# The first layer's gate third of the conditioning matrix: loaded and multiplied inside the in-projection instead of the prologue

## Chip, cores and metric

The kernel runs on one core of a Trainium2 chip. The metric is the device time of one execution in microseconds (us); the program is one launch, and the figures below are of executions of it. TensorE is called PE here, VectorE DVE, ScalarE ACT, GpSimd POOL, and SyncE, which issues the loads, SP.

## What is computed

One inference step of a four-layer decoder: 512 prompt tokens and 8 sample tokens, width 1024. Every layer is a token mixer (layers 0 and 3: a gated short convolution) and a gated convolution FFN. Each of the two is wrapped in norms that are steered by a conditioning vector of 9 sequences:

```
mod = jnp.einsum('bd,lde->lbe', jax.nn.silu(c), p['ada_w']) + p['ada_b'][:, None, :]
...
sh_m, sc_m, gt_m, sh_f, sc_f, gt_f = jnp.split(mod[l][:, None, :], N_MOD, axis=-1)
u = rmsnorm(h, p['norm_g'][l, 0]) * (1 + sc_m) + sh_m
...
out, nb = short_conv_mixer(u, st_conv_a[j], p['sconv_w_in'][j], p['sconv_conv_w'][j],
                           p['sconv_w_out'][j])
...
h = h + gt_m * rmsnorm(out, p['norm_g'][l, 1])
```

So of the matrix half that belongs to a layer's mixer, shift and scale (`sh_m`, `sc_m`) are needed before the layer's first matmul, and the gate (`gt_m`) only after its out-projection.

## The kernel before

**The conditioning matrix.** `ada_w` is 1024 rows by 6144 columns for each layer, in f32. A half of it (3072 columns, index h from 0 to 7) serves one sub-layer, a third of a half is 1024 columns: shift, scale or gate. The half h = 0 is needed first of all and is handled in the prologue: SP issues six loads of 2 MB (`ada_pro`, line 546), each 512 columns wide, and PE multiplies each as it comes (line 1782, 32 matmuls of 128 columns a step, steps 0 to 5). A step's sums go through DVE (`mod_rows`, line 2565) and back through a small PE matmul (line 1788) into `ada_ps` in PSUM. Between these steps PE also forms the statistics of the first norm (line 1717), and turns the vectors of biases and gains, which DVE copies to `vecs` (lines 2568 and 2569). Then `modulation(0, 0, mod_m)` adds bias and gain on DVE (lines 2535, 2537, 2542).

**The other halves** come in pieces of 128 rows by 1024 columns (512 KB), two to a pair, into a buffer `ada_raw` that holds one pair. A pair costs PE 8 matmuls (line 1628). Eight pieces, four pairs, make one third; then ACT copies the sums out of PSUM (`copy_sums`, line 1029, into `acc_sb`) and PE turns them into `ada_ps` (`turn_sums`, line 1621) before the next third's first pair. The half h = 1 (12 pairs) is spread over the in-projection of layer 0.

**The in-projection** ("sconv") of layer 0 multiplies 24 blocks of weights, 1024 by 128 each, called B0 to B23 here, with the normed input, in 4 iterations of two tiles (e = 0 and 1) of 3 blocks. A block is loaded by SP into one of two slots of `w_raw` (`load_block`, line 504), copied by ACT to `w_hi` (`high`, line 981), subtracted by POOL to `w_lo` (`low`, line 765; in parts for the first two, line 772), and then multiplied on PE: high parts (line 1667), low part (line 1675). B0 and B1 are multiplied together, as the normed input comes out of ACT and DVE (`gemm_pair`, lines 1690 and 1696).

**What sets the order.** Each engine runs its own list of instructions in order, and waits at the head of it. On SP a load of a pair waits until PE has used the pair before it (`ada_used`), and a load of a block waits until POOL is done with the block two before it (`lo_done`). On PE `conv_tile` places the pairs behind blocks: one pair behind each odd block, so B1, B3, B5 and so on. On ACT `conv_tile` copies the sums behind the weight copy that the pair is near to (`sums_behind`).

## Time and profile before

| | |
|---|---|
| median of 3 runs | 3019.37 us (3018.94 to 3023.8) |
| span of the profiled execution | 3014.3 us |
| PE busy | 2876.1 us, 95% of the span |
| weight loads on PE (PEld) busy | 2733.3 us, 91% |
| DVE, ACT, POOL busy | 51%, 36%, 44% |
| DMA | 332.56 MB, 110 GB/s on average |

The span runs from the first instruction to the last of one execution; the median lies 5.1 us above it. Times in rows are microseconds from the start of that span. PE is the engine that is full almost everywhere; the change concerns the first 210 us, where the profile shows the prologue (to about 53 us) and the in-projection of layer 0 (to about 210 us).

### The profile page before, as it was taken

What the parts mean: (1) busy time and instruction counts of PE and PEld (TensorE: products, weight loads), DVE (VectorE), ACT (ScalarE), POOL (GpSimd) and SP (SyncE); (2) the same over time, 40 slices, a digit from 0 to 9 for tenths busy, and PEclk for the clock granted to TensorE, in tenths of its full rate; (3) what the DMA queues carried; (4) which work ended last, traced back from release to release, by engine and by line L of the source; (5) the groups of instructions that cost most, each with busy time, mean ns of one, the idle gap of its engine ahead of it and who ended that gap; (6) DMA issues with size and microseconds to landing.
All of it is one profiled execution on the core that took longest, in us unless ns stands there. A gap on an engine that the chain in (4) does not pass through costs nothing.

```text
span 3014.3 us, 72962 instructions
## 1 busy us (share of the span) xinstructions
PE 2876.1 (95%) x29617; PEld 2733.3 (91%) x29617; DVE 1528.4 (51%) x2080; ACT 1085.0 (36%) x2139; POOL 1321.5 (44%) x959
## 2 busy tenths in 40 slices
PE   6999999998989999999998999999999999899998
PEld 5998999997978877899997899889999899799998
DVE  3435666118357874666603242476650444566612
ACT  4224333225455652433323444343332422433322
POOL 3443444442435554344443273434444344344443
PEclk9999999999999999999999999999999999899999
DMA  7544333544411013333354323533334543133332
GB/s 269 164 151 159 95 92 88 158 128 136 119 44 32 4 37 124 120 89 92 99 159 152 99 64 112 169 123 89 92 116 146 173 120 91 57 92 92 91 91 85
DMA packets 465618, 332.56 MB, mean 110 GB/s; under 512 B 19914, under 2 KB 435608, under 8 KB 465122
## 3 DMA queue, kind: packets, MB, share of 16 engines
q1 hardware_dynamic: 461400, 325.24, 35.1%
q10 hardware_dynamic: 4010, 4.22, 0.6%
q8 instruction: 172, 2.82, 0.4%
q14 instruction: 36, 0.29, 0.0%
HBM read 319.62 MB, written 10.20 MB: 109 GB/s over the span
## 4 chain that ended last, share of the span: by engine, by line
PE 62%; DVE 4%; ACT 2%; issue 1%; DMA 1%; SPq 0%; POOL 0%; ACTq 0%; DVEq 0%
PE banks L1667 33%; PE banks L1675 16%; PE banks L2126 5%; PE banks L2133 1%; PE banks L1628 1%; PE banks L1973 1%; DVE h L2662 1%; PE banks L1690 1%; DVE proj L2606 1%; PE banks L1761 0%; DMA s_state<-in_state_wkv_b_dram 0%; ACT conv L1080 0%; PE banks L2135 0%; ACT uv L1433 0%; DVE proj_b L2606 0%
## 5 line engine op out<-in xcount | busy, mean ns | idle before, releaser
L765 POOL TENSOR_TENSOR w_lo<-w_raw,w_hi 128x1024 fp32r<-128x1024 f32 x395 | 1007.5, 2551 | 1108.1 <-ACT w_hi L981 1088.0
L1667 PE MATMUL banks<-u_hi,w_hi 128*128 128x260 f32 x4064 | 834.5, 287 | 14.2 <-ACT w_hi L981 9.4
L1667 PE MATMUL banks<-u_lo,w_hi 128*128 128x260 f32 x4064 | 825.1, 284 | 0.0
L1667 PEld LDWEIGHTS banks<-u_hi,w_hi 128*128 128x128 f32 x4064 | 627.4, 189 | 27.1 <-issue 15.2
L1667 PEld LDWEIGHTS banks<-u_lo,w_hi 128*128 128x128 f32 x4064 | 629.9, 189 | 1.6
L981 ACT ACTIVATE w_hi<-w_raw 128x1024 fp32r<-128x1024 f32 x402 | 424.5, 1056 | 454.2 <-PE banks L1675 284.4
L1675 PE MATMUL banks<-u_hi,w_lo 128*128 128x260 f32 x4064 | 527.5, 282 | 0.0
L1675 PEld LDWEIGHTS banks<-u_hi,w_lo 128*128 128x128 f32 x4064 | 502.1, 187 | 1.3
L1667 PE MATMUL banks<-hid_hi,w_hi 128*128 128x260 f32 x1664 | 336.3, 283 | 0.0
L1667 PE MATMUL banks<-hid_lo,w_hi 128*128 128x260 f32 x1664 | 335.2, 283 | 0.0
L3113 DVE TENSOR_TENSOR csb<-proj 128x520 f32 (+1 forms) x42 | 30.3, 722 | 470.8 <-ACT proj L1048 470.8
L2594 DVE TENSOR_TENSOR hid_lo<-prod,hid_hi 128x520 f32 x104 | 259.7, 2497 | 12.8
L1667 PEld LDWEIGHTS banks<-hid_hi,w_hi 128*128 128x128 f32 x1664 | 256.8, 188 | 5.0 <-issue 3.7
L2578 DVE SCALAR_TENSOR_TENSOR conv<-gate,vecs,conv 128x536 f32<-128x536 f32 x104 | 249.2, 2396 | 15.1 <-DVE conv L2576 0.8
L1667 PEld LDWEIGHTS banks<-hid_lo,w_hi 128*128 128x128 f32 x1664 | 256.1, 188 | 0.0
L1675 PE MATMUL banks<-hid_hi,w_lo 128*128 128x260 f32 x1664 | 217.0, 282 | 0.0
L1675 PEld LDWEIGHTS banks<-hid_hi,w_lo 128*128 128x128 f32 x1664 | 206.4, 188 | 0.0
L780 POOL TENSOR_TENSOR tail<-gate,ones 128x2 f32<-128x2 f32 x104 | 28.0, 269 | 339.1 <-ACT gate L1536 339.1
L1543 ACT ACTIVATE conv<-conv,vecs 128x536 f32<-128x536 f32 x88 | 65.5, 744 | 287.5 <-DVE conv L2578 287.5
L2575 DVE TENSOR_SCALAR conv<-gate,vecs 128x536 f32<-128x536 f32 x104 | 55.9, 538 | 194.5 <-ACT gate L1536 190.5
L1534 ACT ACTIVATE gate<-banks 128x260 f32<-128x260 f32 x88 | 34.1, 387 | 256.2 <-PE banks L1675 254.8
L2576 DVE SCALAR_TENSOR_TENSOR conv<-gate,vecs,conv 128x536 f32<-128x536 f32 x104 | 108.1, 1039 | 15.2 <-DVE conv L2575 1.7
(463 smaller groups left out, 3898.8 us busy)
## 6 DMA issues: line engine op xcount, KB each, us to landing
w_raw<-in_ffn_w_up_dram SPq DMA_DIRECT2D x176, 512.0 KB, 3.7
ada_raw<-in_ada_w_dram SPq DMA_DIRECT2D x96, 512.0 KB, 4.7
w_raw<-in_ffn_w_down_dram SPq DMA_DIRECT2D x64, 448.0 KB, 3.7
w_raw<-in_sconv_w_in_dram SPq DMA_DIRECT2D x48, 512.0 KB, 5.2
ada_ahead<-in_ada_w_dram SPq DMA_DIRECT2D x36, 512.0 KB, 7.7
ada_ahead_down<-in_ada_w_dram SPq DMA_DIRECT2D x36, 512.0 KB, 6.2
w_raw<-in_ffn_w_down_dram SPq DMA_DIRECT2D x32, 512.0 KB, 4.0
ada_pro<-in_ada_w_dram SPq DMA_DIRECT2D x6, 2048.0 KB, 21.2
```

Of the source, the lines that this page charges most:

```text
L765: pool.tensor_tensor(w_lo[:, s, :, :], w_raw[:, s, :, :], w_hi[:, s, :, :].bitcast(F32), ALU.subtract).then_inc(lo_done, 1)
L981: act.activation(w_hi[:, s, :, :], w_raw[:, s, :, :], ACT.Copy).then_inc(hi_done, 1)
L1534: act.activation(gate[:, e, 2:2 + HALF], tile_ps[0][0][:, 0:HALF], ACT.Copy)
L1543: act.activation(conv[:, e, 0:CWD], conv[:, e, 0:CWD], ACT.Silu, bias=vec("ffn_conv_b", l * FT + m)).then_inc(silu_done, 1)
L1667: pe.matmul(tile_ps[slot][half][0:width, 0:HALF], w_hi[:, s, k, 0:width], x[:, k0 + k, half * HALF:(half + 1) * HALF], start=start and k = ...
L1675: mm = pe.matmul(tile_ps[slot][half][0:width, 0:HALF], w_lo[:, s, k, 0:width], xh[:, k0 + k, half * HALF:(half + 1) * HALF], start=False, ...
L2126: mm = pe.matmul(out(rs), left(rs), right(rs), start=start, stop=stop)
L2575: link(dve.tensor_scalar(conv[:, e, 0:CWD], gate[:, e, 0:CWD], w[0], None, ALU.mult))
L2576: link(dve.scalar_tensor_tensor(conv[:, e, 0:CWD], gate[:, e, 1:1 + CWD], w[1], conv[:, e, 0:CWD], ALU.mult, ALU.add))
L2578: dve.scalar_tensor_tensor(conv[:, e, 0:CWD], gate[:, e, 2:2 + CWD], w[2], conv[:, e, 0:CWD], ALU.mult, ALU.add).then_inc(conv_done, 1)
L2594: dve.tensor_tensor(lo, prod[:, e, :], hi.bitcast(F32), ALU.subtract).then_inc(hid_ready, 1)
L3113: return dve.tensor_tensor(csb[:, 1, :], o, o, ALU.mult)
```

## The change

Of the half h = 0 the prologue now loads and multiplies only shift and scale (four steps instead of six). The gate third is cut into pieces like the other halves: four more pairs, called P0 to P3 here, go through `ada_raw`; the twelve pairs of h = 1 are P4 to P15. The in-projection of layer 0 now places a pair behind the first block of each iteration and behind each odd block: four pairs an iteration. ACT copies a third's sums at the end of each iteration. The gate's sums are turned into PSUM bank 7 and finished on DVE after the in-projection.

```diff
@@ prologue
+PRO_STEPS = 2 * KT // PRO_T
...
-            for i in range(GT // PRO_T):
-                if i == len(ada_pro):
-                    sp.wait_ge(pro_mod_mm, 1)
+            for i in range(PRO_STEPS):
                 sp.dma_start(ada_pro[i % len(ada_pro)][:, :, :], w[:, :, i * PRO_T * P:(i + 1) * PRO_T * P])\
                   .then_inc(ada_pro_loaded[i], 16)
@@ SP
+            def load_first_gate(x):
+
+                for s in range(2):
+                    i = 2 * KT + 2 * x + s
+                    sp.wait_ge(ada_used, i + 1)
+                    sp.dma_start(ada_raw[:, s, :], ada_columns(0, i)).then_inc(ada_loaded[s], 16)
...
                                 load_block(n0 + 6 * it + k, k % 2, w[:, :, ds((part * KT + m) * P, P)])
...
-                                if k % 2:
-                                    load_ada_slot(p, 3 * it + k // 2)
+                                if l:
+                                    if k % 2:
+                                        load_ada_slot(p, 3 * it + k // 2)
+                                elif k == 0 or k % 2:
+                                    x = 4 * it + (k + 1) // 2
+                                    if x < FIRST_GATE:
+                                        load_first_gate(x)
+                                    else:
+                                        load_ada_slot(p, x - FIRST_GATE)
@@ ACT, conv_tile
                             high(n + i, (k + i) % 2)
-                            if i == 3 - e:
+                            if l and i == 3 - e:
                                 sums_behind(p, 3 * it + e)
-                        if e:
+                        if l and e:
                             sums_behind(p, 3 * it + 2)
+                        if l == 0 and e:
+                            copy_sums(it - 1)
                         rows_to_dram(q, q0 // 2 + it, e,
@@ PE
-            pe.sem_inc(ada_used, 2 + GT)
+            pe.sem_inc(ada_used, 2 + 2 * KT)
...
             def turn_sums(group, first_tile):
-                pe.wait_ge(acc_copied, group + 1)
+                pe.wait_ge(acc_copied, group + 2)
+                sums = first_gate_ps if group < 0 else ada_ps
...
-            for i in range(GT // PRO_T + 1):
+            for i in range(PRO_STEPS + 1):
...
-                            if k % 2:
-                                ada_slot(p, 3 * it + k // 2)
+                            if l:
+                                if k % 2:
+                                    ada_slot(p, 3 * it + k // 2)
+                            elif k == 0 or k % 2:
+                                first_layer_slot(4 * it + (k + 1) // 2)
                         turn_tail(q, e)
+
+                    def first_layer_slot(x):
+
+                        if x < FIRST_GATE:
+                            for s in range(2):
+                                pe.wait_ge(ada_loaded[s], 16 * x + 16)
+                                ada_columns(ada_raw[:, s, :], 2 * x + s)
+                        else:
+                            if x == FIRST_GATE:
+                                pe.wait_ge(rows_copied, q0 + 3)
+                            ada_slot(p, x - FIRST_GATE)
@@ DVE
-            modulation(0, 0, mod_m)
+            def first_modulation():
+
+                dve.wait_ge(mod_mm, 2 * KT)
+                bias = vecs[:, col["ada_b"]:col["ada_b"] + 2 * KT].unsqueeze(2).to_broadcast([P, 2 * KT, NSEQ])
+                gain = vecs[:, col["norm_g"]:col["norm_g"] + KT].unsqueeze(2).to_broadcast([P, KT, NSEQ])
+                scale = mod_m[:, KT:2 * KT, :]
+                link(dve.tensor_tensor(mod_m[:, 0:2 * KT, :], ada_ps[:, 0:2 * KT * NSEQ].rearrange("p (t s) -> p t s", s=NSEQ),
+                                       bias, ALU.add))
+                link(dve.tensor_scalar(scale, scale, 1.0, None, ALU.add))
+                dve.tensor_tensor(scale, scale, gain, ALU.mult).then_inc(mod_ready, 1)
+                dve.wait_ge(mod_ready, 1)
+
+            def first_gate():
+
+                dve.wait_ge(mod_mm, GT)
+                dve.wait_ge(rows_copied, KT + 1)
...
+                link(dve.tensor_tensor(gate_rows, gate_rows, gain, ALU.mult))
+
+            first_modulation()
...
                     after_loop(b, s, PER, p["iters"])
+                    if l == 0:
+                        first_gate()
                     modulation(l, 1, mod_f)
```

SP's list at the start of layer 0, before the change. `ada_pro` are the last three of the prologue's 2 MB loads, `w_raw` blocks of weights (x2: two in a row), `ada_raw` the two pieces of a pair, `st_in` a small state load:

```order
L546 DMA ada_pro_203<-in_ada_w_dram 128x8x512
L546 DMA ada_pro_204<-in_ada_w_dram 128x8x512
L546 DMA ada_pro_200<-in_ada_w_dram 128x8x512
L540 DMA st_in<-in_state_conv_a_dram 16x128
L504 DMA w_raw<-in_sconv_w_in_dram 128x8x128 x2
L519 DMA ada_raw<-in_ada_w_dram 128x1024 x2
L504 DMA w_raw<-in_sconv_w_in_dram 128x8x128
L540 DMA st_in<-in_state_conv_a_dram 16x128
L504 DMA w_raw<-in_sconv_w_in_dram 128x8x128
L519 DMA ada_raw<-in_ada_w_dram 128x1024 x2
```

The same place on SP with the change (`ada_raw` at line 557 are the gate third's pairs P0, P1, P2):

```order
L548 DMA ada_pro_203<-in_ada_w_dram 128x8x512
L544 DMA st_in<-in_state_conv_a_dram 16x128
L508 DMA w_raw<-in_sconv_w_in_dram 128x8x128
L557 DMA ada_raw<-in_ada_w_dram 128x1024 x2
L508 DMA w_raw<-in_sconv_w_in_dram 128x8x128
L557 DMA ada_raw<-in_ada_w_dram 128x1024 x2
L508 DMA w_raw<-in_sconv_w_in_dram 128x8x128
L544 DMA st_in<-in_state_conv_a_dram 16x128
L508 DMA w_raw<-in_sconv_w_in_dram 128x8x128
L557 DMA ada_raw<-in_ada_w_dram 128x1024 x2
```

The first pair now stands between B0 and B1, and a second one, P1, stands ahead of B2, where before no pair stood between B2 and the pair behind B1.

SP's list at the end of the first iteration and the start of the second, before (the first `w_raw` x2 are B4 and B5, the last one is B8):

```order
L504 DMA w_raw<-in_sconv_w_in_dram 128x8x128 x2
L519 DMA ada_raw<-in_ada_w_dram 128x1024 x2
L540 DMA st_in<-in_state_conv_a_dram 16x128
L504 DMA w_raw<-in_sconv_w_in_dram 128x8x128 x2
L519 DMA ada_raw<-in_ada_w_dram 128x1024 x2
L504 DMA w_raw<-in_sconv_w_in_dram 128x8x128
```

The same with the change (line 557 is P3, line 523 is P4 and P5):

```order
L508 DMA w_raw<-in_sconv_w_in_dram 128x8x128 x2
L557 DMA ada_raw<-in_ada_w_dram 128x1024 x2
L544 DMA st_in<-in_state_conv_a_dram 16x128
L508 DMA w_raw<-in_sconv_w_in_dram 128x8x128
L523 DMA ada_raw<-in_ada_w_dram 128x1024 x2
L508 DMA w_raw<-in_sconv_w_in_dram 128x8x128
L523 DMA ada_raw<-in_ada_w_dram 128x1024 x2
L508 DMA w_raw<-in_sconv_w_in_dram 128x8x128
```

B6 and B7 stood together; now P4 stands between them, and P5 between B7 and B8.

ACT's list at the end of an iteration in which a third's sums are copied, before (the weight copies, the copy of the sums, the output rows and the next tile's first copies out of PSUM):

```order
L981 ACTIVATE w_hi<-w_raw 128x1024 x2
L1029 ACTIVATE acc_sb<-banks 128x256
L981 ACTIVATE w_hi<-w_raw 128x1024
L994 ACTIVATE rows<-banks 10x128
L996 DMA out_conv_a_prompt_dram<-rows 2x128
L997 DMA out_conv_a_sample_dram<-rows 8x128
```

The end of the first iteration with the change (the three weight copies are B5, B6 and B7):

```order
L997 ACTIVATE w_hi<-w_raw 128x1024 x3
L1045 ACTIVATE acc_sb<-banks 128x256
L1010 ACTIVATE rows<-banks 10x128
L1012 DMA out_conv_a_prompt_dram<-rows 2x128
L1013 DMA out_conv_a_sample_dram<-rows 8x128
```

The copy of the sums now stands behind all three weight copies, B7's being the last.

## Rows read from the trace of the kernel before

**Rows 1.** The page: busy time, share of the span and instructions of PE

```profile
PE 2876.1 (95%) x29617; PEld 2733.3 (91%) x29617; DVE 1528.4 (51%) x2080; ACT 1085.0 (36%) x2139; POOL 1321.5 (44%) x959
```

**Rows 2.** Stretches: length, busy us (count) by engine, clock, DMA share, GB/s

```profile
40.00:50.00 10.00, 5.84 (x122) 4.92 (x110) 2.90 (x6) 2.11 (x2) 2.83 (x5) 0.83 0.94 315
50.00:60.00 10.00, 7.20 (x43) 6.94 (x44) 9.01 (x17) 7.89 (x11) 2.68 (x4) 0.66 0.36 106
100.00:120.00 20.00, 20.00 (x183) 18.63 (x182) 6.75 (x11) 5.75 (x11) 8.76 (x5) 1.00 0.40 122
```

**Rows 3.** Timeline, prologue: start, length, engine, line, operation [idle before, releaser]

```profile
17.75 1.95 PE L1782 MATMUL banks<-ada_pro,cT 128*32 128x128 f32 x64 [1.76 <-ACT h L975]
...
22.29 3.15 PE L1782 MATMUL banks<-ada_pro,cT 128*32 128x128 f32 x64 [2.58 <-DMA ada_pro<-in_ada_w_dram]
...
35.28 1.95 PE L1782 MATMUL banks<-ada_pro,cT 128*32 128x128 f32 x64
...
38.10 0.48 DVE L2569 COPY vecs<-banks 128x318 f32<-128x318 f32 x1
...
39.39 3.19 PE L1782 MATMUL banks<-ada_pro,cT 128*32 128x128 f32 x64 [1.82 <-DMA ada_pro<-in_ada_w_dram]
...
44.70 1.95 PE L1782 MATMUL banks<-ada_pro,cT 128*32 128x128 f32 x64 [1.54 <-DMA ada_pro<-in_ada_w_dram]
46.03 1.06 ACT L981 ACTIVATE w_hi<-w_raw 128x1024 fp32r<-128x1024 f32 x1 [14.02 <-DMA w_raw<-in_sconv_w_in_dram]
...
47.17 5.50 POOL L772 TENSOR_TENSOR w_lo<-w_raw,w_hi 128x256 fp32r<-128x256 f32 x8 [31.27 <-ACT w_hi L981]
47.54 1.06 ACT L981 ACTIVATE w_hi<-w_raw 128x1024 fp32r<-128x1024 f32 x1 [0.45 <-DMA w_raw<-in_sconv_w_in_dram]
47.58 0.38 DVE L2535 TENSOR_TENSOR mod_m<-banks,vecs 128x216 f32<-128x216 f32 x1 [0.56 <-PE banks L1788]
...
48.67 1.36 DVE L2542 TENSOR_TENSOR mod_m<-mod_m,vecs 128x72 f32<-128x72 f32 x2
...
50.07 0.22 DVE L2623 TENSOR_TENSOR s<-h,banks 128x64 f32<-128x64 f32 x1
...
53.24 0.77 PE L1690 MATMUL banks<-u_hi,w_hi 128*128 128x260 f32 x2 [2.71 <-DVE u_lo L2637]
```

**Rows 4.** Timeline of PE: the first pair, B2, and what follows B2

```profile
66.53 1.07 PE L1628 MATMUL banks<-ada_raw,cT 128*32 128x256 f32 x16
68.15 0.48 PE L1667 MATMUL banks<-u_hi,w_hi 128*128 128x260 f32 x2 [0.55 <-ACT w_hi L981]
...
73.97 0.27 PE L1710 MATMUL banks<-ident,tail 128*10 128x128 f32 x1
```

**Rows 5.** Timeline of SP's queue: issues of loads (start, time to issue)

```profile
49.97 0.38 SPq L504 DMA_DIRECT2D w_raw<-in_sconv_w_in_dram  x1
...
93.37 0.81 SPq L519 DMA_DIRECT2D ada_raw<-in_ada_w_dram  x2
94.23 0.43 SPq L504 DMA_DIRECT2D w_raw<-in_sconv_w_in_dram  x1
```

**Rows 6.** DMA issues of 94.2 to 94.6: count, size, us from issue to landing

```profile
w_raw<-in_sconv_w_in_dram SPq DMA_DIRECT2D x1, 512.0 KB, 6.0
```

**Rows 7.** Timeline of PE: a pair, the next block, a turn of sums with its pair

```profile
92.67 1.07 PE L1628 MATMUL banks<-ada_raw,cT 128*32 128x256 f32 x16
...
93.81 0.49 PE L1667 MATMUL banks<-u_hi,w_hi 128*128 128x260 f32 x2
...
118.26 0.53 PE L1621 MATMUL banks<-ident,acc_sb 128*128 128x36 f32 x4
118.72 1.07 PE L1628 MATMUL banks<-ada_raw,cT 128*32 128x256 f32 x16
```

**Rows 8.** Timeline of ACT: a weight copy and the copy of a third's sums

```profile
105.63 1.06 ACT L981 ACTIVATE w_hi<-w_raw 128x1024 fp32r<-128x1024 f32 x1 [4.17 <-PE banks L1675]
106.60 0.39 ACT L1029 ACTIVATE acc_sb<-banks 128x256 f32<-128x256 f32 x1
```

More of the change, by code:

```diff
@@ L259, in trunk_kernel @@
         st_ps, acc_ps, ada_ps, tail_ps = bank[4], bank[6][:, 2 * P:4 * P], bank[6], bank[7]
+        first_gate_ps = bank[7][:, 2 * P:4 * P]
         sums_ps = bank[4]
@@ L278, in trunk_kernel @@
         pro_mod_mm, pro_mod_copied = sem("pro_mod_mm"), sem("pro_mod_copied")
-        ada_pro_loaded = [sem(f"ada_pro_loaded{i}") for i in range(GT // PRO_T)]
+        ada_pro_loaded = [sem(f"ada_pro_loaded{i}") for i in range(6)]
         ada_used = sem("ada_used")
@@ L467, in in_norms @@
             return 2 <= h < HALVES
+        FIRST_GATE = KT // 2
         def pair_of(p, slot):
@@ L474, in raw_turn @@
         def raw_turn(h, pair):
-            return pair if h == 1 else GT // 2 + (h - 2) * 6 + {3: 0, 7: 1}.get(pair, pair - 6)
+            return FIRST_GATE + pair if h == 1 else FIRST_GATE + GT // 2 + (h - 2) * 6 + {3: 0, 7: 1}.get(pair, pair - 6)
         def ahead_of(h):
@@ L1612, in _ @@
                 pe.sem_inc(s, 2)
-            pe.sem_inc(ada_used, 2 + GT)
+            pe.sem_inc(ada_used, 2 + 2 * KT)
             row_groups = ident[:, :].rearrange("p (g c) -> p g c", g=NG)[:, :, 0:NSEQ]
             def turn_sums(group, first_tile):
-                pe.wait_ge(acc_copied, group + 1)
+                pe.wait_ge(acc_copied, group + 2)
+                sums = first_gate_ps if group < 0 else ada_ps
                 for i in range(2):
-                    pe.matmul(ada_ps[:, ds((first_tile + i * NG) * NSEQ, NG * NSEQ)], acc_sb[:, i * P:(i + 1) * P],
+                    pe.matmul(sums[:, ds((first_tile + i * NG) * NSEQ, NG * NSEQ)], acc_sb[:, i * P:(i + 1) * P],
                               row_groups, start=True, stop=True).then_inc(mod_mm, NG)
@@ L1642, in ada_slot @@
                 h = p["ada"] // GT
-                if pair and pair % (KT // 2) == 0:
+                if pair % (KT // 2) == 0 and (pair or h == 1):
                     group = pair // (KT // 2) - 1
-                    turn_sums((h - 1) * (GT // KT) + group, group * KT)
+                    turn_sums((h - 1) * (GT // KT) + group, max(group, 0) * KT)
                 for s in range(2):
@@ L1655, in ada_ahead @@
                 else:
-                    pe.wait_ge(ada_pro_loaded[i % KT], 16 * (2 * (h - 2) + i // KT + 2))
+                    pe.wait_ge(ada_pro_loaded[i % KT], 16 * (2 * (h - 2) + i // KT + (2 if i % KT < PRO_STEPS else 1)))
                     ada_columns(ahead_of(h)[i % KT][:, :], i % KT)
@@ L1775, in _ @@
                     statistics(0)
-                if i < GT // PRO_T:
+                if i < PRO_STEPS:
                     pe.wait_ge(ada_pro_loaded[i], 16)
@@ L2557, in spread @@
                 return rstd_ps[1].unsqueeze(1).to_broadcast([P, KT, NS])
-            for i in range(GT // PRO_T):
+            for i in range(PRO_STEPS):
                 if i == SUM_STEP:
@@ L2569, in _ @@
                     link(dve.tensor_copy(vecs[:, 512:nrow], bank[3][:, 0:nrow - 512]))
-            modulation(0, 0, mod_m)
+            def first_modulation():
[11 more added lines that the diff above has]
+                dve.wait_ge(rows_copied, KT + 1)
+                c0 = col["ada_b"] + 2 * KT
+                bias = vecs[:, c0:c0 + KT].unsqueeze(2).to_broadcast([P, KT, NSEQ])
+                c0 = col["norm_g"] + KT
+                gain = vecs[:, c0:c0 + KT].unsqueeze(2).to_broadcast([P, KT, NSEQ])
+                gate_rows = mod_m[:, 2 * KT:3 * KT, :]
+                link(dve.tensor_tensor(gate_rows, first_gate_ps[:, 0:KT * NSEQ].rearrange("p (t s) -> p t s", s=NSEQ), bias,
+                                       ALU.add))
+                link(dve.tensor_tensor(gate_rows, gate_rows, gain, ALU.mult))
+            first_modulation()
             def conv3(q, e, name, row0, m, ft):
```

## The prediction

> **What bounds the kernel now.** I read the page first: PE is busy for 95% of the span [rows 1], so a microsecond counts only where PE waits or where work is added to PE. The stretches show where that is. In the in-projection PE has no gap at all (20.00 of 20 us at clock 1.00), while in the last part of the prologue it is 58% busy and the DMA engines carry 315 GB/s at a share of 0.94 [rows 2]. The change takes load and work out of the second place and puts them into the first. So I went to the timeline of the prologue for what the change can save, and to the timelines of PE, SP and ACT in the in-projection for what it costs.
>
> In the prologue the steps on `ada_pro` wait for data: the step at 22.29 and the one at 44.70 both start when a load lands, and they are four loads apart, so one load of 2 MB takes (44.70 - 22.29) / 4 = 5.6 us [rows 3]. Two chains then meet at the first pair of blocks at 53.24. One is the modulation: last step at 44.70, first DVE operation at 47.58, first use of its result at 50.07, first matmul 3.17 us behind that. The other is the weights: B0 is copied at 46.03, B1 at 47.54, POOL subtracts both in 5.50 us and ends at 52.67 [rows 3]. Neither is far ahead of the other.
>
> **Part 1, the prologue: -9.7 us.** Steps 4 and 5 go, the last step is the one at 35.28, which waited for no data. DVE then finishes the vectors at 38.58 (38.10 + 0.48) and can start the modulation there, against 47.58: 9.0 us earlier. One of the two multiplications of L2542 also goes, half of 1.36 us, so the result is used at 50.07 - 9.7 = 40.4 and the pair could start at 43.6 [rows 3]. The weights: two loads less bring them 11.2 us earlier, but P0 (1 MB, half of 5.6) now stands ahead of B1. B1's copy comes at 47.54 - 11.2 + 2.8 = 39.1, and POOL, which needs 2.75 us for each block, ends with it at about 43.0. That is 0.6 us before the modulation is through, so the gain is 9.7 us. Bounds: 11.2 if nothing but the two loads counted, 8.4 if B1's later place sets the start (5.7 us from 47.54 to 53.24, as before). The first pair itself I leave as long as it is, 53.24 to 66.53 [rows 3, 4].
>
> **Part 2, a hole behind the first pair: +7.0 us.** Before, PE goes from P0's place at 66.53 to B2 at 68.15, in 1.62 us [rows 4]; B2's load had been issued at 49.97 [rows 5]. Now P1 stands directly behind P0 on PE, and on SP ahead of B2. P1 goes into the buffer that P0 holds, so SP cannot issue it before PE has used P0, and B2's load, B3's and a state load queue behind that wait, though their slots are free. How long such a sequence takes stands in the trace: a pair used at 92.67 lets SP issue the next pair at 93.37 (0.70 later) and a weight block at 94.23 (0.86 later), which lands 6.0 us after its issue [rows 5 to 7]. ACT's copy takes 1.06 [rows 8]. B2 thus starts 0.70 + 0.86 + 6.0 + 1.06 = 8.6 us after P0, against 1.62. P1's multiplication lies inside this. Nothing covers it: PE has no other work at its head. Lower bound: the 1.5 MB at the full rate of the prologue take 4.2 us from the issue, so B2 starts 6.0 us after P0, and the hole costs 4.3.
>
> **Part 3, the clock: +1.8 us behind the hole, and 1.5 at the turns below.** After the wait that ended at 53.24 the first stretch ran at a granted clock of 0.66 on average [rows 2], that is, 6.8 us at 1.2 GHz, of which some 3.6 were matmuls. In the prologue the step behind a wait of 2.58 us took 3.15 us and the one behind 1.82 us took 3.19, while those behind 1.76 and 1.54 us took 1.95 [rows 3]. So behind a hole of 7 us I take the loss of the first pair again, half of 3.6, 1.8, with 1.24 and twice that as bounds. A wait of about 2 us lies between rows that lost nothing and rows that lost 1.24; for three of them I take 1.5 together (0 to 3.7).
>
> **Part 4, more work for PE: +3.7 us.** Four pairs of 1.07 us at most are added to a stretch in which PE has no gap; one lies in the hole, so 3.2. One turn of sums more is 0.46 (118.26 to 118.72) [rows 7]. What PE no longer does in the prologue (two steps of 1.95) lay beside the loads and is already in part 1.
>
> **Part 5, the turns from one iteration to the next: +7.9 us.** Let S be when PE begins an iteration's fourth pair. The next pair's load waits for that use, B7's load queues behind it (then B13's, B19's), and lands at S + 0.70 + 0.86 + 6.0 = S + 7.6. ACT's copy of the sums stands behind B7's weight copy, since ACT works in order; from the start of such a copy to the end of the copied sums the trace has 105.63 to 106.99, 1.36 us [rows 8]. The sums are there at S + 8.9. PE needs them before the next pair, and comes there at S + 1.14 (92.67 to 93.81) + 5.82 (one block, 68.15 to 73.97) = S + 6.96 [rows 4, 7]. It waits 1.96 us. Behind that pair's use SP issues P5 and only then B8, so B8 is ready 8.6 us after the pair began, and PE is through with the pair, B7 and P5 after 1.07 + 5.82 + 1.07 = 7.96: 0.66 more. Three turns (after iterations 1, 2, 3): 3 x 2.62 = 7.9. Bounds: 0 if the loads ran at the full rate, and 3 x 4.6 if the first wait came twice at each turn (a rival, below).
>
> DVE's two additional operations for the gate come after the last tile, where DVE waits for PE in any case; its old two of the same size took 1.36 us with the vectors [rows 3]. I cost them at nothing; without that cover they would be 1 us.
>
> **Sum.** -9.7 + 7.0 + 1.8 + 1.5 + 3.7 + 7.9 = +12.2 us. Against the profiled span, 3014.3 + 12.2 = 3026.5; the median of the runs lies 5.1 us above that span, and I carry it over: 3019.4 + 12.2 = 3031.6.
>
> **The rivals.**
>
> *The loads are covered* (not slower). Place: SP's queue in the in-projection, where the DMA engines have a share of 0.40 [rows 2]. If the four new pairs land while PE multiplies, only PE's own work is paid: -9.7 + 4 x 1.07 + 0.46 = -5.0, so 3014.4. It decides from the point at which a pair's issue and the block behind it fit into PE's work in between; that is 6.96 us of PE work against 8.9 at the turns, and nothing at all against 8.6 behind the first pair. For it speaks the idle DMA; against it the order, in which P1 cannot be issued earlier. 6%. This is what the Trainium skill would have of such a change (DMA: Bandwidth & Descriptors, Rules for kernel authors): it advises issuing a DMA early and waiting late, so that its fixed cost lies beside compute. The rows agree for a load that is issued early, as B2's at 49.97, and not for one that waits for its buffer.
>
> *The loads run at the full rate* of the prologue. Then part 2 is 4.3, part 5 nothing, and the turns' 1.5 us of clock go: -9.7 + 4.3 + 1.8 + 3.7 = +0.1, so 3019.5. Against it: the 6.0 us were measured in this very sequence of loads [rows 6]. 11%.
>
> *The delay runs on.* ACT takes the tile of B6 out of PSUM after the copy of the sums, and DVE's gate and the next blocks' copies come later too. If each turn holds PE up once more by 1.96: +5.9, so 3037.5 or above. For it: ACT, SP and PE each wait in order here. Against it: behind B8 the old distance of two blocks between pairs is back, 11.6 us of PE work. 13%.
>
> The clock is no rival of its own: if every turn's wait lost 1.24 us, the sum would be 3033.8. [...] The rows show both outcomes behind waits of this size.
>
> **How the numbers follow.** The forecast has 70%, with its bounds 3025 to 3037. The predicted time is 3031.6. The range reaches from 3023, which leaves out the two quicker rivals (17%), to 3039, which takes in most of the delay that runs on. About 0.2% (6 us) is what a measurement of this kernel can tell from no change, so "slower" begins at 3025.4 and "faster" ends at 3013.3: slower 0.70 + 0.13 less a little of the forecast's lower end, 0.81; same 0.16, mostly the rival at the full rate and part of the covered one; faster 0.03, the better half of the covered one.
>
> **What would show it.** The first matmul of the first pair at about 43.6 (part 1). A hole in PE of 6 to 7 us, broken by P1's matmuls, before B2, with SP's load of B2 issued some 1.5 us after P0's use (part 2), and a clock of 0.5 behind it (part 3). Three waits of PE for `acc_sb` of about 2 us each, and after each a shorter one for `w_hi` of the block two further on (part 5). I would be wrong if B2's load were issued during the first pair, if ACT copied the sums before B7's weights, or if the pair started much before 42.

## The result and the profile after

| | before | after |
|---|---|---|
| median | 3020.22 us (3018.94 to 3024.18) | 3030.06 us (3028.62 to 3033.07) |
| span of the profiled execution | 3014.3 us | 3026.9 us |
| mean granted clock of PE in it | 0.979 | 0.977 |

The changed kernel is slower: the ratio of the medians is 1.0031, 95% interval 1.0021 to 1.0042, so 6.3 to 12.7 us at 3020. The profiled span grew by 12.6 us.

The page's line of the engines of the changed kernel, to be read beside [rows 1]:

```profile
PE 2881.5 (95%) x29553; PEld 2735.2 (90%) x29553; DVE 1524.7 (50%) x2079; ACT 1084.4 (36%) x2140; POOL 1318.4 (44%) x959
```

PE's busy time rose by 5.4 us only (2876.1 to 2881.5), the span by 12.6. The rest is waiting. To see where, the same stretches as in [rows 2], with one more around the third turn (length, busy us and count of PE, PEld, DVE, ACT, POOL, granted clock, DMA share, GB/s):

```profile
40.00:50.00 10.00, 6.65 (x33) 6.68 (x34) 9.08 (x15) 7.96 (x12) 2.77 (x4) 0.66 0.00 0
...
60.00:70.00 10.00, 5.12 (x33) 3.79 (x34) 1.80 (x3) 2.11 (x2) 3.46 (x2) 0.66 0.87 305
100.00:120.00 20.00, 17.06 (x155) 15.69 (x156) 7.04 (x11) 5.60 (x11) 9.31 (x6) 1.00 0.68 211
180.00:200.00 20.00, 18.05 (x151) 16.27 (x150) 3.50 (x7) 4.34 (x8) 5.39 (x3) 0.91 0.67 203
```

The stretch from 40 to 50, which carried 315 GB/s before, now carries nothing: the prologue's loads are over. The stretch from 60 to 70 looks like the old prologue: the DMA engines are full (305 GB/s) and PE is busy for half of it, at a clock of 0.66. And 100 to 120, without a gap before, has 2.94 us of them.

**The prologue** answers to [rows 3]. Timeline of the changed kernel (start, length, engine, line, operation, idle before and releaser): DVE's first step of the modulation, B1's weight copy, POOL's second subtraction, the first pair.

```profile
38.49 0.31 DVE L2610 TENSOR_TENSOR mod_m<-banks,vecs 128x144 f32<-128x144 f32 x1
...
39.09 1.06 ACT L997 ACTIVATE w_hi<-w_raw 128x1024 fp32r<-128x1024 f32 x1 [2.90 <-DMA w_raw<-in_sconv_w_in_dram]
...
40.22 2.77 POOL L788 TENSOR_TENSOR w_lo<-w_raw,w_hi 128x256 fp32r<-128x256 f32 x4 [1.17 <-ACT w_hi L997]
...
43.35 0.77 PE L1709 MATMUL banks<-u_hi,w_hi 128*128 128x260 f32 x2 [3.59 <-DVE u_lo L2696]
```

The pair starts at 43.35 instead of 53.24: 9.89 us earlier. POOL ends with B1's low part at 42.99, so both chains are through within 0.4 us of each other, as the prediction had it.

**The hole behind the first pair** answers to [rows 4, 5]. PE of the changed kernel: P0, P1 in its two pieces, B2, and what follows B2.

```profile
57.58 1.07 PE L1647 MATMUL banks<-ada_raw,cT 128*32 128x256 f32 x16
62.15 0.64 PE L1647 MATMUL banks<-ada_raw,cT 128*32 128x256 f32 x8 [3.50 <-DMA ada_raw<-in_ada_w_dram]
63.46 1.08 PE L1647 MATMUL banks<-ada_raw,cT 128*32 128x256 f32 x8 [0.67 <-DMA ada_raw<-in_ada_w_dram]
66.60 0.77 PE L1686 MATMUL banks<-u_hi,w_hi 128*128 128x260 f32 x2 [2.07 <-ACT w_hi L997]
...
73.81 0.27 PE L1729 MATMUL banks<-ident,tail 128*10 128x128 f32 x1
```

SP's queue in the same place (start of the issue, its time): P1's two loads and B2's.

```profile
58.28 0.80 SPq L557 DMA_DIRECT2D ada_raw<-in_ada_w_dram  x2
59.13 0.43 SPq L508 DMA_DIRECT2D w_raw<-in_sconv_w_in_dram  x1
```

The DMA issues of 59.1 to 59.5 (count, size, us from issue to landing):

```profile
w_raw<-in_sconv_w_in_dram SPq DMA_DIRECT2D x1, 512.0 KB, 6.2
```

SP issues P1 0.70 us after P0's use began, and B2 only behind it, 1.55 us after P0. B2's load lands 6.2 us after its issue, at 65.3, ACT copies it, and PE begins B2 at 66.60, 9.02 us after P0 where it was 1.62 [rows 4]: +7.40. B2 itself took 7.21 us instead of 5.82, with the clock low for its first 3 us (two of its matmuls take 0.64 us until 69.3, and 0.41 from 69.75 on): +1.39. So at the end of B2 the changed kernel stands at 73.81 against 73.97: of 9.89 us gained, 0.16 are left.

**The turns.** PE of the changed kernel around the first one: the fourth pair (P3), the turn of sums, P4, P5, B8.

```profile
92.52 1.07 PE L1647 MATMUL banks<-ada_raw,cT 128*32 128x256 f32 x16
...
101.44 0.61 PE L1640 MATMUL banks<-ident,acc_sb 128*128 128x36 f32 x4 [1.79 <-ACT rows L1010]
101.98 1.07 PE L1647 MATMUL banks<-ada_raw,cT 128*32 128x256 f32 x16
...
108.91 1.07 PE L1647 MATMUL banks<-ada_raw,cT 128*32 128x256 f32 x16
111.48 0.48 PE L1686 MATMUL banks<-u_hi,w_hi 128*128 128x260 f32 x2 [1.50 <-ACT w_hi L997]
```

SP's queue ahead of that turn: the loads of the next pair (P4) and B7's.

```profile
93.22 0.81 SPq L523 DMA_DIRECT2D ada_raw<-in_ada_w_dram  x2
94.07 0.43 SPq L508 DMA_DIRECT2D w_raw<-in_sconv_w_in_dram  x1
```

ACT in that place: B7's weight copy, the copy of the sums, the output rows.

```profile
99.87 1.06 ACT L997 ACTIVATE w_hi<-w_raw 128x1024 fp32r<-128x1024 f32 x1 [11.40 <-DMA w_raw<-in_sconv_w_in_dram]
100.83 0.36 ACT L1045 ACTIVATE acc_sb<-banks 128x256 f32<-128x256 f32 x1
101.09 0.25 ACT L1010 ACTIVATE rows<-banks 10x128 f32<-10x128 f32 x1
```

SP issues P4 0.70 us after P3's use began and B7 behind it; B7's load lands 5.8 us after its issue. ACT had been idle for 11.40 us when B7's weights came, and the sums stood behind them. All of PE's longer waits between 40 and 230 us, grouped (line, waited for: us in total, times, longest):

```profile
PE banks L1686 <- ACT w_hi L997: 4.3, 3, 2.1
PE banks L1647 <- DMA ada_raw<-in_ada_w_dram: 4.2, 2, 3.5
PE banks L1640 <- ACT acc_sb L1045: 4.0, 3, 2.0
PE banks L1709 <- DVE u_lo L2696: 3.6, 1, 3.6
PE banks L1640 <- ACT rows L1010: 1.8, 1, 1.8
```

The first and second rows hold the hole (2.07, and 3.50 + 0.67) and the weights' part of two turns (1.50 + 0.69); the third and fifth the sums' part of three turns (1.79, 1.69, 1.95) and 0.39 at the end of the in-projection, which was there before, too. The second and third turn, on PE:

```profile
144.82 0.61 PE L1640 MATMUL banks<-ident,acc_sb 128*128 128x36 f32 x4 [1.69 <-ACT acc_sb L1045]
...
154.05 0.48 PE L1686 MATMUL banks<-u_hi,w_hi 128*128 128x260 f32 x2 [0.69 <-ACT w_hi L997]
```

```profile
187.92 0.61 PE L1640 MATMUL banks<-ident,acc_sb 128*128 128x36 f32 x4 [1.95 <-ACT acc_sb L1045]
188.46 1.31 PE L1647 MATMUL banks<-ada_raw,cT 128*32 128x256 f32 x16
...
196.92 1.07 PE L1647 MATMUL banks<-ada_raw,cT 128*32 128x256 f32 x16
```

After the third wait the clock fell: from the pair to the next pair it is 8.46 us (188.46 to 196.92) where the first turn took 6.93 (101.98 to 108.91), 1.53 more.

**The end of the in-projection** serves as a yardstick from here on: the last turn of sums on PE, before the change and after it.

```profile
210.10 0.60 PE L1621 MATMUL banks<-ident,acc_sb 128*128 128x36 f32 x4 [0.39 <-ACT acc_sb L1029]
```

```profile
224.12 0.61 PE L1640 MATMUL banks<-ident,acc_sb 128*128 128x36 f32 x4 [0.39 <-ACT acc_sb L1045]
```

It comes 14.02 us later. The rest of the span is 1.4 us shorter (2804.2 before, 2802.8 after), so the whole loss lies in the in-projection.

### The profile page after: what moved, and what is told of

Same layout as the page of the kernel before. It is cut to its first block, busy times and chain, and to the rows that moved or that the text cites. A ratio compares the mean times of both kernels' runs of the same rounds, so it can differ in the third digit from the quotient of the medians.

```text
span 3026.9 us, 72839 instructions
## 1 busy us (share of the span) xinstructions
PE 2881.5 (95%) x29553; PEld 2735.2 (90%) x29553; DVE 1524.7 (50%) x2079; ACT 1084.4 (36%) x2140; POOL 1318.4 (44%) x959
## 4 chain that ended last, share of the span: by engine, by line
PE 62%; DVE 4%; ACT 2%; issue 1%; DMA 0%; POOL 0%; ACTq 0%; DVEq 0%
PE banks L1686 33%; PE banks L1694 17%; PE banks L2159 4%; PE banks L2166 1%; PE banks L1647 1%; PE banks L2006 1%; DVE h L2721 1%; DVE proj L2665 1%; PE banks L1709 1%; PE banks L1780 0%; DMA s_state<-in_state_wkv_b_dram 0%; ACT conv L1096 0%; PE banks L2168 0%; ACT uv L1451 0%; PE banks L1736 0%
```

## Experiments

The theory is the prediction's: the pairs cost little as work and much by their place. P1's load, waiting for its buffer, holds B2's load back on SP's queue (the hole), and the load of the pair behind an iteration's end holds B7's back, behind whose copy ACT's copy of the sums stands (the turns). The rivals: the pairs' work and the traffic themselves cost what was lost, wherever they stand; or ACT's order alone does.

All edits are to the changed kernel. The unchanged kernel before ran on the same chip in the same stretch of time: median 3019.38 us beside the first four, 3018.44 beside the last four. The table gives the places on PE's timeline (us) and the medians; "sums" is the last turn of sums.

| kernel | first pair | P0 | B2 | sums | median | ratio to before, interval |
|---|---|---|---|---|---|---|
| before | 53.24 | (66.53) | 68.15 | 210.10 | | |
| changed | 43.35 | 57.58 | 66.60 | 224.12 | 3030.06 | 1.0031 [1.0021, 1.0042] |
| changed, once more | 43.72 | 56.66 | 65.60 | 224.48 | 3032.84 | 1.0045 [1.0032, 1.0058] |
| no gate third | 42.36 | (56.30) | 57.92 | 199.83 | 3007.05 | 0.9965 [0.9953, 0.9978] |
| SP's order | 43.74 | 57.17 | 64.05 | 211.86 | 3019.72 | 1.0002 [0.9992, 1.0011] |
| sums earlier on ACT | 43.82 | 57.37 | 66.19 | 221.30 | 3029.69 | 1.0034 [1.0021, 1.0047] |
| sums and rows earlier on ACT | 43.54 | 57.80 | 66.68 | 217.69 | 3024.29 | 1.0021 [1.0012, 1.0030] |
| first iteration spread | 41.92 | 56.18 | 57.80 | 217.11 | 3023.99 | 1.0017 [1.0009, 1.0026] |
| pairs spread | 42.83 | 56.09 | 57.71 | 204.91 | 3012.33 | 0.9980 [0.9971, 0.9989] |
| P0 ahead of the first pair | 43.35 | 39.55 | 59.12 | 204.78 | 3011.36 | 0.9975 [0.9965, 0.9985] |

(In brackets: the pair of h = 1 that stands in that place where there is no P0.)

**The changed kernel once more.** No edit; a second profile shows how far the places repeat from one execution to another.

> The changed kernel once more, unaltered, beside the three below on the same chip. Theory: 3030, 10 to 11 us above the kernel before; the same waits of PE in the in-projection as in its first profile (9.0 us behind the first pair of blocks, about 2 us at each of three turns). Rival (the first profile's waits depend on where the clock's low stretches fall): waits of another length at the turns.

The waits came again (turns 1.67, 1.71, 1.84 us; the hole 8.94 us from P0 to B2), and the last turn of sums within 0.4 us, at 224.48. What did not repeat is the first pair, which took 12.94 us (43.72 to 56.66) against 14.23 (43.35 to 57.58): its matmuls ran at the lower of the two levels of PE's clock for the first 3.0 us of it, and for 6.1 the first time. And B2 took 8.02 us (65.60 to 73.62) against 7.21. The median is 14.4 us above before here (interval 9.7 to 17.5), more than the 10 to 11 expected; it was 9.8 (6.3 to 12.7) the first time.

**No gate third.** The prologue's part alone: four steps, the twelve pairs of h = 1 in their old places.

```diff
-        FIRST_GATE = KT // 2
+        FIRST_GATE = 0
...
-                            if l:
-                                if k % 2:
-                                    ada_slot(p, 3 * it + k // 2)
-                            elif k == 0 or k % 2:
-                                first_layer_slot(4 * it + (k + 1) // 2)
+                            if k % 2:
+                                ada_slot(p, 3 * it + k // 2)
...
-                        first_gate()
+                        link(dve.memset(mod_m[:, 2 * KT:3 * KT, :], 0.0))
```

> The gate third is neither loaded nor multiplied (the gate is set to zero on DVE, so that part of the result is left out); the prologue has four steps as in the changed kernel, and the in-projection has its twelve pairs where they stood before the change. Theory (the prologue gains what the shorter load is worth, and the whole loss is made in the in-projection): the first pair of blocks starts at 43.3 to 43.6 instead of 53.24, no new wait of PE behind it, time 3020.2 - 9 = 3011, 9 to 10 us below the kernel before. Rival (the gain of the prologue is eaten at once, since the first pair of blocks is paced by ACT and DVE or runs longer at the low clock): within 3 us of the kernel before, 3017 or above.

```profile
199.83 0.61 PE L1631 MATMUL banks<-ident,acc_sb 128*128 128x36 f32 x4 [0.39 <-ACT acc_sb L1038]
```

The last turn of sums on PE without the gate third. The first pair starts 10.9 us earlier than before, and the last turn of sums comes 10.27 us earlier. The saving in the prologue is real and is kept to the end when nothing is put in its place: the median is 12.3 us below before, where 9 to 10 were expected. The first pair's start is a little over the -9.7 of the prediction, since here no P0 stands ahead of B1: where P0's load is left out or stands behind B1's, the first pair starts at 41.92 to 42.83, and at 43.35 to 43.82 in the six profiles in which it stands ahead. Everything above 199.83 in the other kernels is the price of the gate third, but for the 1 us or so by which the first pair's length varies: 24.3 us in the changed one.

**SP's order alone.** The same places on PE and ACT, but on SP each pair's load is issued behind weight blocks that would otherwise have waited for it.

```diff
+        PAIR_AFTER = {0: 0, 3: 1, 4: 2, 5: 3, 7: 4, 8: 5, 9: 6, 11: 7, 13: 8, 14: 9, 15: 10, 17: 11, 19: 12, 20: 13, 21: 14,
+                      23: 15}
...
-                                elif k == 0 or k % 2:
-                                    x = 4 * it + (k + 1) // 2
-                                    if x < FIRST_GATE:
+                                else:
+                                    x = PAIR_AFTER.get(6 * it + k)
+                                    if x is not None and x < FIRST_GATE:
                                         load_first_gate(x)
-                                    else:
+                                    elif x is not None:
                                         load_ada_slot(p, x - FIRST_GATE)
```

> The changed kernel with only SP's list in another order: each pair's load stands behind the weight blocks that are needed before or right after it, never ahead of them (P1 behind B3, P4 behind B7, P5 behind B8 and so on). PE, ACT and DVE as in the changed kernel. Theory (the weight blocks are late because they queue on SP behind a pair's wait): the waits of PE at the three turns vanish (1.8 + 1.5, 1.7 + 0.7, 2.0 us, and 1.7 of low clock), the hole behind the first pair shrinks from 9.0 to about 6.5 us, since P1 still waits for P0's buffer; time 3030.1 - 10 to 12 = 3018 to 3020. Rival (the extra traffic or the copy of the sums on ACT makes the waits, whatever SP's order): within 3 us of the changed kernel, 3027 or above.

PE with SP's new order: P0, P1, the start of B2, and the first turn of sums.

```profile
57.17 1.07 PE L1649 MATMUL banks<-ada_raw,cT 128*32 128x256 f32 x16
61.56 1.08 PE L1649 MATMUL banks<-ada_raw,cT 128*32 128x256 f32 x8 [3.32 <-DMA ada_raw<-in_ada_w_dram]
63.04 1.08 PE L1649 MATMUL banks<-ada_raw,cT 128*32 128x256 f32 x8 [0.39 <-DMA ada_raw<-in_ada_w_dram]
64.05 0.80 PE L1688 MATMUL banks<-u_hi,w_hi 128*128 128x260 f32 x2
...
97.43 0.53 PE L1642 MATMUL banks<-ident,acc_sb 128*128 128x36 f32 x4
```

B2 no longer waits and starts 6.88 us behind P0 (6.5 was expected), and at the first turn PE has no wait at all, nor at the second and third (137.34 and 177.26). ACT's list is untouched: it is still in the old order, and that costs nothing once B7's weights come in time. P1 keeps its own wait of 3.32 + 0.39 us, since its load cannot start before P0 is used. The sums are 12.26 us earlier than in the changed kernel for the same work and the same bytes, so the rival by which work and traffic cost it falls: the order of one queue carries most of the loss. The median equals the kernel before.

**The copy of the sums earlier on ACT.** SP as in the change; ACT copies the sums ahead of the last weight copy of iterations 1 to 3.

```diff
-                        if l == 0 and e:
+                            if l == 0 and e and ahead and i == 3:
+                                copy_sums(it - 1)
...
+                        if l == 0 and e and not ahead:
                             copy_sums(it - 1)
```

> The changed kernel with only ACT's list altered: at the end of iterations 1 to 3 the sums are copied ahead of the weight copy of the iteration's last block (B7, B13, B19) instead of behind it; SP and PE as in the changed kernel. Theory (at the turns PE waits for the sums because ACT stands at a weight copy whose load is late): the waits for the sums, 1.8, 1.7 and 2.0 us, go, and in their place come 0.2 to 0.5 us for B7's own copy and 0.5 for B8's; the hole behind the first pair stays; time 3030.1 - 4 to 6 = 3024 to 3026. Rival (B7's late load is what PE waits for, and the sums only stand before it): PE waits the same 2 us for the weight copy, 3029 or above.

This missed: 3029.69 us, hardly less than the change. ACT and PE at its first turn:

```profile
94.42 0.38 ACT L1045 ACTIVATE acc_sb<-banks 128x256 f32<-128x256 f32 x1 [5.30 <-PE banks L1649]
100.60 1.06 ACT L997 ACTIVATE w_hi<-w_raw 128x1024 fp32r<-128x1024 f32 x1 [5.80 <-DMA w_raw<-in_sconv_w_in_dram]
101.56 0.25 ACT L1010 ACTIVATE rows<-banks 10x128 f32<-10x128 f32 x1
```

```profile
101.91 0.61 PE L1642 MATMUL banks<-ident,acc_sb 128*128 128x36 f32 x4 [1.50 <-issue]
```

The sums are copied at 94.42, 7.5 us before PE turns them, and PE still waits 1.50 us. At this one turn it waits for something else as well: ahead of the first pair of h = 1 the code waits for `rows_copied`, that is, for ACT's copy of output rows at 101.56, which stands behind B7's weights just as the sums did. The profile can only call it "issue". At the second and third turn, where there is no such wait, PE had none for the sums (144.47, 185.53), and 0.78 and 0.47 us for the weights of the block behind the next pair. The last turn of sums is no more than 2.8 us earlier, also because the clock fell behind the wait of 1.50: from the pair to the next pair it is 8.50 us (102.45 to 110.95) instead of 6.93, at a clock of 0.70 from 101 to 105. A gain of 2.8 us can't be told from none by the median, whose interval is 8 us wide. The rival was that PE would wait the same 2 us for the weight copies: the time fits it, but the waits for them were 0.68, 0.78 and 0.47 us.

**Sums and output rows earlier on ACT.** The repair of the run before: both stand ahead of the weight copy.

```diff
...
+                            if l == 0 and e and ahead and i == 3:
+                                copy_sums(it - 1)
+                                tile_rows()
...
-                        rows_to_dram(q, q0 // 2 + it, e,
...
+                        if l or not e or not ahead:
+                            tile_rows()
```

> As the kernel with the early copy of the sums, and the tile's output rows, for which PE waits at the first turn as well, are copied ahead of B7's weights too (ACT's list alone is altered). Theory (at the turns PE waits for ACT, which stands at a weight copy): no wait of PE for sums or rows at any of the three turns, up to 0.8 us for a weight copy in their place; the in-projection ends at 217 to 219.5 us of the span instead of 224; time 4 to 6 us below the changed kernel. Rival (PE waits as long for B7's weights): the in-projection ends at 223 or later, time within 2 us of the changed kernel.

```profile
99.61 0.53 PE L1647 MATMUL banks<-ident,acc_sb 128*128 128x36 f32 x4
...
109.72 0.48 PE L1693 MATMUL banks<-u_hi,w_hi 128*128 128x260 f32 x2 [1.56 <-ACT w_hi L997]
```

PE at the first turn: no wait before the turn of sums, as at the other two (141.25, 182.24). Behind P5 the wait for B8 stays (1.56, then 0.51 and 0.40 at the later turns): that one comes from SP's order, which ACT can't mend. The last turn of sums is at 217.69, 6.8 us earlier than in the changed kernel's second profile, and the median 8.6 us lower (3032.84 to 3024.29), where 4 to 6 were expected. So the turns' waits were ACT's order and SP's order together: either one undone takes the wait for the sums away.

**The first iteration spread.** The hole alone is taken away: in the first iteration the four pairs stand behind B1, B2, B4 and B5 on PE, and P1's load behind B3's on SP.

```diff
+        PAIRS_AFTER = {1: (0,), 3: (1,), 4: (2,), 6: (3, 4), 7: (5,), 9: (6,), 11: (7,), 12: (8,), 13: (9,), 15: (10,),
+                       17: (11,), 18: (12,), 19: (13,), 21: (14,), 23: (15,)}
...
-                            elif k == 0 or k % 2:
+                            elif it == 0 and k in (1, 2, 4, 5):
+                                first_layer_slot((1, 2, 4, 5).index(k))
+                            elif it and (k == 0 or k % 2):
                                 first_layer_slot(4 * it + (k + 1) // 2)
```

> The changed kernel with only the first iteration's four pairs spread (P0 to P3 behind B1, B2, B4 and B5, P1's load behind B3); the three turns as in the changed kernel. Theory (the hole behind the first pair and the low clock behind it cost 7.4 + 1.4 us by themselves): B2 starts 1.6 us after P0 instead of 9.0, the waits at the turns stay at 1.7 to 2.0 us and 0.5 to 1.5 us; the in-projection ends at 215 to 216 us; time 3030 - 9 = 3021, 8 to 9 us below the changed kernel. Rival (what is saved there is waited for at the next pairs): the in-projection ends at 220 or later, time less than 4 us below the changed kernel.

```profile
56.18 1.07 PE L1649 MATMUL banks<-ada_raw,cT 128*32 128x256 f32 x16
57.80 0.48 PE L1688 MATMUL banks<-u_hi,w_hi 128*128 128x260 f32 x2 [0.55 <-ACT w_hi L999]
...
63.70 1.07 PE L1649 MATMUL banks<-ada_raw,cT 128*32 128x256 f32 x16
```

PE: P0, B2, P1. B2 is again 1.62 us behind P0, as in [rows 4], and the turns keep their waits (1.69 and 1.51 at the first; 1.74 and 0.39, and 1.96, later). The sums come 7.4 us earlier than in the changed kernel's second profile (at 217.11; 215 to 216 was expected), the median is 8.9 us lower (3032.84 to 3023.99). The hole's price is read where the work is equal: from the start of P0 until P0, P1 and B2 are done it is 8.59 us here (56.18 to 63.70, and P1's 1.07) and 16.96 in the changed kernel's second profile (56.66 to 73.62), 8.4 more; in its first it was 16.23, 7.6 more. The prediction had 7.0 for the hole and 1.8 for the clock behind it, less the 1.07 of P1 that the hole covers: 7.7. Some of the gain is lost again further on: PE now waits 1.04 us for POOL's tail just ahead of the last turn of sums.

**All pairs spread.** Every iteration's pairs behind its second, third, fifth and sixth block, and each pair's load on SP behind the block that needs to be there first.

```diff
+        PAIR_AFTER = {1: 0, 3: 1, 4: 2, 6: 3, 7: 4, 9: 5, 10: 6, 12: 7, 13: 8, 15: 9, 16: 10, 18: 11, 19: 12, 21: 13, 22: 14}
...
+                        if l == 0 and b == 0:
+                            load_ada_pair(1, GT // 2 - 1)
...
-                            elif k == 0 or k % 2:
-                                first_layer_slot(4 * it + (k + 1) // 2)
+                            elif k in (1, 2, 4, 5):
+                                first_layer_slot(4 * it + (1, 2, 4, 5).index(k))
```

> The whole work of the changed kernel, with the sixteen pairs behind the second, third, fifth and sixth block of each iteration (so at least one block between two pairs, P0 behind B1, P1 behind B2), and each pair's load on SP behind the second block after its predecessor's place. Theory (moving the third pays in the prologue and costs only PE's own work, if no load of weights stands behind a pair's wait): no wait of PE above 0.5 us in the in-projection; -9.9 for the start of the first pair, +0.9 for its longer low clock, +4.0 for four pairs, +0.5 for a turn of sums: 3020.2 - 4.5 = 3015.7, 3014 to 3017. Rival (the pairs' traffic in the in-projection costs by itself, by slower loads of weights): above 3020, with PE waiting for weight copies throughout.

All of PE's longer waits between 40 and 230 us in this kernel:

```profile
PE banks L1727 <- DVE mod_m L2616: 2.4, 1, 2.4
PE banks L1712 <- DVE u_lo L2699: 1.8, 1, 1.8
PE banks L1689 <- ACT w_hi L1000: 0.6, 1, 0.6
PE banks L1643 <- ACT acc_sb L1048: 0.4, 1, 0.4
PE banks L1650 <- DMA ada_raw<-in_ada_w_dram: 0.2, 1, 0.2
```

The first two are the prologue's end; 0.6 and 0.4 were there before the change, and 0.2 is left of what it brought. The last turn of sums is at 204.91. Against the kernel without the gate third that is 5.08 us for the whole gate third, and its work is four pairs of 1.07 and a turn of 0.53, 4.8. So the loads of the moved third can be hidden whole, 6 us behind their issue or not, if nothing that is needed sooner stands behind them in the queue and a block of PE's work lies between two pairs. This kernel is faster than both: 3012.33 us, 0.2% below before (3014 to 3017 was expected).

**P0 ahead of the first pair.** As the last one, but P0 is multiplied while PE waits for the first pair's operands, and P1 to P3 stand behind B1, B3 and B5.

```diff
+        PAIR_AFTER = {0: 0, 1: 1, 3: 2, 5: 3, 7: 4, 9: 5, 10: 6, 12: 7, 13: 8, 15: 9, 16: 10, 18: 11, 19: 12, 21: 13, 22: 14}
...
                             if first and i == 0:
+                                if l == 0:
+                                    first_layer_slot(0)
...
```

> As the spread version, but P0 is multiplied ahead of the first pair of blocks, where PE waits for the modulation and the weights, and P1 to P3 stand behind B1, B3 and B5. Theory (PE is idle from 38 to 43 us, so P0's 1.07 us cost nothing there): the first pair of blocks starts as early as in the spread version, the in-projection ends 1.0 us sooner, about 204; time 1 us below the spread version, 3010 to 3013. Rival (P0's load or its matmuls delay the first pair of blocks): the first pair starts 1 us later or more and nothing is gained, 3012 to 3015.

```profile
43.35 0.56 PE L1712 MATMUL banks<-u_hi,w_hi 128*128 128x260 f32 x1 [2.73 <-POOL w_lo L791]
```

PE: P0 does lie in the wait (39.55 to 40.62), but the first pair now waits for POOL's low part and starts at 43.35, against 42.83 when all pairs are spread. For P0's load stands ahead of B1's, and ACT copies B1 at 39.00 instead of 36.50. The last turn of sums is 0.13 us earlier (204.78), not the whole pair (1.0 was expected); the medians of the two, 3011.36 and 3012.33, each beside its own before, are not told apart.

## Why the prediction was right, term by term

The forecast was 3031.6 us, 12.2 above before; the medians say 9.8 (14.4 the second time), the profiled spans 12.6. The 5.1 us from the profiled span to the median, which the prediction carried over, were 3.2 with the change. Its terms against the two traces:

| term | predicted | traces |
|---|---|---|
| 1, prologue: start of the first pair | -9.7 | -9.89 |
| length of the first pair | 0 | +0.94 |
| 2, hole behind it | +7.0 | +7.40 |
| 3, clock behind the hole | +1.8 | +1.39 |
| 4, three pairs and a turn of sums | +3.7 | +3.7, from the same durations |
| 5, waits at the turns | +7.9 | +7.62 |
| 3, clock at the turns | +1.5 | +1.53, all at one turn |
| left over in the in-projection | | +1.3 |
| behind the in-projection | 0 | -1.4 |
| sum | +12.2 | +12.6 |

**Part 1** held in its size and in its reason. Two loads and two steps less, and both chains through at about 43 us.

**The first pair** was costed as unchanged and took 0.94 us more. It is not the change: the same stretch took 12.94 us in the changed kernel's other profile, 13.26 with all pairs spread, and 14.26 in two further ones (43.54 to 57.80, 41.92 to 56.18), against 13.29 before. An unchanged stretch behind a wait has that spread, and it goes with the time at the lower level of the clock: 3.9 us of it before, 6.1 in the changed kernel, 3.0 in its other profile.

**Part 2** held step by step: 0.70 us to SP's next issue, 0.85 more to B2's (59.13 against 58.28), 6.2 to the landing where 6.0 was taken from [rows 6], and then the copy. The full-rate bound of 4.3 us did not come about; the load that SP issued third in a row landed 5.8 to 6.7 us after its issue in four places (6.0 before; 6.2, 5.8 and 6.7 with the change). The clock behind the hole cost 1.39 us, and 2.20 in the second profile, on both sides of the predicted 1.8. The Trainium skill's advice to issue a DMA early and to wait late (DMA: Bandwidth & Descriptors, Rules for kernel authors) agrees with the kernel with all pairs spread, where the same loads cost PE 0.2 us; in the changed kernel B2's load could not be issued early, because it stood behind one that couldn't.

**Part 5** has the right sum out of partly wrong pieces. The first wait was to come at S + 8.9 and came there: S is 92.52, the turn of sums 101.44. But what ended it at the first turn was the copy of the output rows, not of the sums; the prediction had not read that PE also waits for `rows_copied` ahead of the first pair of h = 1. In the changed kernel this is worth some 0.2 us, since ACT copies the rows right behind the sums, but it is what made the experiment with the sums alone miss. And the second wait, for B8's, B14's and B20's weights, was to be 0.66 each time and was 1.50, 0.69 and none. At the first turn B8's load took 6.7 us to land, where 6.0 was assumed; at the third PE was late itself, at the low clock, and the weights were there.

**The clock at the turns** was costed at half a loss for each of three waits of 2 us. It came once whole (1.53 us behind the wait of 1.95, more than the 1.24 of the prediction's row) and not at all behind 1.79 and 1.69. In the second profile of the change the granted clock was 0.91 in both 140 to 160 and 180 to 200, so which waits lose it differs from execution to execution.

**The rivals.** That the loads are covered, and that they run at full rate, both fall with the hole and the turns' waits. That the delay runs on does as well: behind B8 the timeline has no further wait until the next turn. The covered case was not wrong as a mechanism, though: with all pairs spread it is what happens, at 204.91 for the sums, 5.2 us ahead of before, and the prediction's price for it was -5.0.

**What stays open.** About 1.3 us of the in-projection's 14.0 are spread in tenths around the new waits and pairs and were not taken apart. And the differences of the medians from before are lower than those of the last turn of sums, by 0.9 to 4.2 us in eight of nine cases (the changed kernel: +9.8 against +14.0; all pairs spread: -7.1 against -5.2). Whether the rest of the kernel gains a little from the change, or the one profile of before is early by chance, the runs don't tell. The profiles show no such gain: behind the last turn of sums they have 2802.4 to 2811.0 us left, and before, with 2804.2, lies in the midst of them. DVE's operations for the gate, costed at nothing, lie in that part and left no loss that shows. That the sum hit the profiled span within 0.4 us is partly luck: +0.94 and +1.3 were missed, and -1.4 came back behind.

## What to carry to other kernels

A load on a queue that issues in order should stand behind every load whose buffer comes free sooner; one that waits for its buffer passes its wait on to all behind it, and an idle DMA engine doesn't help. Moving a load out of a stretch bound by DMA into one where PE is full pays only what the receiving queue's order lets it: here the same four pairs cost 24.3 us in one order, 12.0 in another, and 5.1 when they were also spread on PE. And before a copy is moved ahead on an engine, look for every wait of the consumer, since the next one in line takes the place of the one removed.

## What was not expected of the hardware

The unchanged kernel's executions beside the experiments range from 3012.55 to 3024.57 us, 0.4%, and a difference of some us can come from where the granted clock falls: the profiles of these kernels have a mean of 0.974 to 0.979, and the changed kernel alone shows both 0.977 and 0.974. A place on the timeline early in the program, such as the last turn of sums, repeated within 0.4 us in the two profiles of the changed kernel and was the sharper yardstick for an edit of this size.

A wait of PE of 1.5 to 2.0 us sometimes lowered the clock for what came behind it and sometimes did not, in the same kernel and place: behind the wait of 1.69 us at 144.82 the changed kernel kept 1.00, and in its other profile the stretch around that turn, with 1.71, was at 0.91. With the sums alone copied earlier, a wait of 1.50 lowered it. Each time it cost about 1.5 us.
